# Turning rows ahead of their norm, halves for the first expert's rows, VectorE in place of GpSimd for low halves, and unread products in TensorE's waits

## What is computed

```
xn = rms_norm(x, norm2_g)
g_logits = xn @ wg + bg                      # 4 groups
g_idx = argmax(g_logits); g_w = softmax(g_logits)[g_idx]
e_logits = (xn @ we + be)[group g_idx]       # 4 experts of that group
top_p, top_i = top_k(softmax(e_logits), 2); top_p /= sum(top_p)
y = sum over the two experts e of g_w * top_p * ((silu(xn @ w_gate[e]) * (xn @ w_up[e])) @ w_down[e])
out = rms_norm(x + y, final_norm_g)
```

## Time and profile before

| | |
|---|---|
| median of 3 runs | 869.72 us |
| profiled execution | 869.15 us, span 867.4 us |
| TensorE busy | 801.0 us (92%) |
| VectorE busy | 495.5 us (57%) |
| ACT busy | 449.2 us (52%) |
| POOL busy | 218.0 us (25%) |
| granted TensorE clock, mean | 0.965 |
| TensorE in the chain that ended last | 81% |

### The profile page before, as it was taken

The page is one execution under the profiler, slowest core; times in us unless marked ns, Lnnn a source line. Parts: engine busy times, 40 slices in busy tenths (PEclk is TensorE's granted clock), DMA queues, the critical chain, the costliest instruction groups (busy, mean ns, idle before and its releaser), DMA issues.

```text
span 867.4 us, 10612 instructions
## 1 busy us (share of the span) xinstructions
PE 801.0 (92%) x3635; PEld 631.7 (73%) x3635; DVE 495.5 (57%) x649; ACT 449.2 (52%) x580; POOL 218.0 (25%) x126
## 2 busy tenths in 40 slices
PE   4999999999979999999999967899999999999960
PEld 3887766676756888888888866688787787877750
DVE  6613647657472222204012435698889898988865
ACT  5244637454552232323222221687888878887842
POOL 5554323132232344444444234000000000000013
PEclk9999999999999999999999967999999999999995
DMA  8665451512120343333328364999999999975945
GB/s 308 179 243 188 128 194 49 194 49 74 40 80 27 89 169 118 99 93 95 98 96 280 131 239 197 366 400 385 405 389 393 408 395 406 389 299 209 367 137 207
DMA packets 126633, 186.76 MB, mean 215 GB/s; under 512 B 9149, under 2 KB 61957, under 8 KB 126597
## 3 DMA queue, kind: packets, MB, share of 16 engines
q1 hardware_dynamic: 119156, 167.82, 54.3%
q10 hardware_dynamic: 5136, 10.08, 3.1%
q0 software_dynamic: 2304, 8.39, 2.7%
HBM read 158.99 MB, written 27.28 MB: 215 GB/s over the span
## 4 chain that ended last, share of the span: by engine, by line
PE 81%; DVE 7%; ACT 4%; issue 3%; DMA 2%; POOL 1%; ACTq 1%; DVEq 0%; SPq 0%
PE ps L947 24%; PE ps L949 23%; PE ps L948 23%; PE ps L1030 3%; PE ps L1010 2%; PE ps L1171 2%; PE ps L1019 1%; DVE w_lo L350 1%; PE ps L1119 1%; ACT w_hi L339 1%; DVE rgate L1394 1%; PE ps L1178 1%; DMA x<-in_x 1%; ACT xn L879 1%; DMA slots<-y_tile 1%
## 5 line engine op out<-in xcount | busy, mean ns | idle before, releaser
L344 POOL TENSOR_TENSOR w_lo<-raw,w_hi 128x1024 fp32r<-128x1024 f32 x72 | 176.2, 2450 | 286.8 <-ACT w_hi L332 286.8
L332 ACT ACTIVATE w_hi<-raw 128x1024 fp32r<-128x1024 f32 x73 | 77.0, 1057 | 169.0 <-PE ps L949 159.9
L947 PE MATMUL ps<-xn_hi,w_hi 128*128 128x512 f32 x352 | 143.8, 409 | 0.0
L949 PE MATMUL ps<-xn_hi,w_lo 128*128 128x512 f32 x352 | 137.5, 390 | 0.0
L948 PE MATMUL ps<-xn_lo,w_hi 128*128 128x512 f32 x352 | 137.3, 390 | 0.0
L947 PE MATMUL ps<-w_hi,xT_hi 128*128 128x512 f32 x256 | 105.2, 411 | 8.1 <-DVE xT_lo L1644 5.5
L948 PE MATMUL ps<-w_lo,xT_hi 128*128 128x512 f32 x256 | 102.3, 399 | 0.0
L949 PE MATMUL ps<-w_hi,xT_lo 128*128 128x512 f32 x256 | 102.2, 399 | 0.0
L947 PEld LDWEIGHTS ps<-xn_hi,w_hi 128*128 128x128 f32 x352 | 66.0, 188 | 26.8 <-issue 13.8
L614 POOL DMA_INDIRECT raw_mg<-slots,slot_idx x7 | 6.9, 982 | 303.6 <-ACTq L930 295.1
L949 PEld LDWEIGHTS ps<-xn_hi,w_lo 128*128 128x128 f32 x352 | 66.1, 188 | 14.4
(11 more groups left out here) (260 smaller groups left out, 1457.5 us busy)
## 6 DMA issues: line engine op xcount, KB each, us to landing
raw<-in_w_in SPq DMA_DIRECT2D x52, 512.0 KB, 3.7
raw_mg<-in_exp_w_down SPq DMA_DIRECT2D x36, 512.0 KB, 8.3
raw<-in_exp_w_gate SPq DMA_DIRECT2D x28, 512.0 KB, 10.3
raw_a<-in_exp_w_gate SPq DMA_DIRECT2D x27, 512.0 KB, 9.8
raw_c<-in_exp_w_up SPq DMA_DIRECT2D x27, 512.0 KB, 9.2
slots<-raw SPq DMA_DIRECT2D x24, 512.0 KB, 6.5
raw_mg<-in_exp_w_up SPq DMA_DIRECT2D x21, 512.0 KB, 9.8
raw<-in_exp_w_up SPq DMA_DIRECT2D x16, 512.0 KB, 9.5
```

The lines of the kernel that those rows point to most:

```text
L332: nc.scalar.activation(w_hi[:, b % HI_SLOTS, :], raw_buf(b), ACT.Copy)\
L344: eng.tensor_tensor(w_lo[:, b % HI_SLOTS, :], raw_buf(b), w_hi[:, b % HI_SLOTS, :].bitcast(F32), ALU.subtract)\
L947: pe.matmul(dst, hi_l, hi_r, start=start, stop=False)
L949: return pe.matmul(dst, lo_l, hi_r, start=False, stop=stop)
```

## The change

1. The rows are turned ahead of their norm. `turn_x2(t)` turns x_rows (not xn2) as soon as x is added, in the middle of the products of tile t+1, and logits(t) follows tile t+1 of w_out. So that the logits come out right, router_w is multiplied by norm2_g once (VectorE, ahead of the additions, from a new load `g2_cols` on ACT's queue), and the logits are multiplied by each row's factor in one more operation. VectorE waits for all six of ACT's loads of the semaphore route_in there.
2. The bookkeeping. The two subtractions for the exponentials and the table of experts stand later in VectorE's list. `picked_bf` comes from one addition. The weights of the choices (`weights`) stand behind the experts.
3. Low halves. POOL makes none for the experts; blocks 0 to 3 of the first expert go to VectorE, behind its routing. SP's fetches of blocks 0 to 2 of tile 2 wait for them there.
4. Tile 0 in halves. The matrix of zeros and ones is made in four operations, one for each token tile. The gathering is made in two halves of four k each, and high and low parts follow in halves; the first two blocks of the expert wait only for the first half's.
5. Unread products. After the last logits 11, after the counts 2, and before and after `turn_x(x_odd)` 8 each, products of the identity by itself (128 x 128 x 128, float32) go into bank 7.

```diff
@@ SP
                 if r == 3:
+                    sp.wait_ge(S["tile0_half"], 2)
                     sp.wait_ge(S["scattered"], 16 * 2 * NT)
@@ POOL
-            for r in range(AHEAD):
-                split_lo(pool, B_EXP + r)
...
-            for r in range(AHEAD, 8 + AHEAD):
-                if r < 8:
-                    if on_pool(r):
-                        split_lo(pool, B_EXP + r)
@@ ACT
                     act.dma_start(g2_rows[:, :], a["norm2_g"][0:1, :].broadcast_to([P, D])).then_inc(S["g2_in"], 16)
+                    act.dma_start(g2_cols[:, :], a["norm2_g"][0].rearrange("(k p) -> p k", p=P),
+                                  allow_slow_non_contiguous=True)\
+                       .then_inc(S["route_in"], 16)
                     act.dma_start(router_w[:, :, 0:NG], a["router_grp_w"][0].rearrange("(k p) n -> p k n", p=P))\
...
-            xT_hi_part(1)
+            act.wait_ge(S["gexp_in"], 1)
+            act.activation(route[:, 4, 0:4 * NG], route[:, 3, 0:4 * NG], ACT.Exp).then_inc(S["gexp_done"], 1)
+            act.wait_ge(S["gexp_in"], 2)
+            act.activation(route[:, 12, :], route[:, 11, :], ACT.Exp).then_inc(S["eexp_done"], 1)
+            for half in range(2):
+                act.wait_ge(S["tile0_half"], half + 1)
+                act.activation(xT_hi[:, 4 * half:4 * half + 4, :].rearrange("p k n -> p (k n)"),
+                               ps[:, 3 + half, :], ACT.Copy).then_inc(S["tile0_hi"], 1)
@@ TensorE
+            def turn_x2(t):
+                pe.wait_ge(S["x2_done"], NT + t + 1)
...
+                                      x_rows[:, t, k * P:(k + 1) * P], ident[:, :])
...
-                if t >= 2:
-                    logits(t - 2)
+                    if kp == 1 and t >= 1:
+                        turn_x2(t - 1)
                 if t >= 1:
-                    turn_xn2(t - 1)
-            turn_xn2(NT - 1)
-            logits(NT - 2)
+                    logits(t - 1)
+            def unread(n):
+
+                for _ in range(n):
+                    pe.matmul(ps[:, 7, 0:P], ident[:, :], ident[:, :], start=True, stop=True)
+
+            turn_x2(NT - 1)
             logits(NT - 1)
+            unread(11)
...
             mm.then_inc(S["counts_ps"], 1)
+            unread(2)
...
+            for half in range(2):
                 for t in range(NT):
...
+                    if half == 0:
+                        pe.wait_ge(S["tile0_where"], t + 1)
+                    for k in range(4 * half, 4 * half + 4):
+                        mm = pe.matmul(ps[:, 3 + half, (k % 4) * P:(k % 4 + 1) * P], xn2[:, t, k * P:(k + 1) * P],
...
             for r in range(8):
+                pe.wait_ge(S["tile0_lo"], 1 if r < 2 else 2)
                 lo_wait(pe, B_EXP + r)
                 expert_block(r % HI_SLOTS, r // 4, 2 * (r % 4), KD, xT_hi, xT_lo)
+            unread(8)
             turn_x(x_odd, S["x_odd_in"], 16)
+            unread(8)
@@ VectorE
             dve.wait_ge(S["g2_in"], 16)
+            dve.wait_ge(S["route_in"], 96)
+            dve.tensor_tensor(router_w[:, :, :], router_w[:, :, :],
+                              g2_cols[:, :].unsqueeze(2).to_broadcast([P, KD, NG + NE]), ALU.mult)\
+               .then_inc(S["router_scaled"], 1)
...
-                                   router_b[:, :].unsqueeze(1).to_broadcast([P, NT, NG + NE]), ALU.add))
+                                   stat[:, 5, :].unsqueeze(2).to_broadcast([P, NT, NG + NE]), ALU.mult))
+            link(dve.tensor_tensor(both, both, router_b[:, :].unsqueeze(1).to_broadcast([P, NT, NG + NE]), ALU.add))
...
+            for t in range(NT):
+                dve.tensor_scalar(silu[:, t * P:(t + 1) * P], hid[:, 0:P], slot0[:, t:t + 1], None, ALU.is_equal)\
+                   .then_inc(S["tile0_where"], 1)
+            dve.tensor_tensor(row(11, NT, NE), e_log, spread(e_max, NT, NE), ALU.subtract).then_inc(S["gexp_in"], 1)
...
+            for half in range(2):
+                split_lo(dve, B_EXP + half)
+                dve.wait_ge(S["tile0_hi"], half + 1)
+                dve.tensor_tensor(xT_lo[:, 4 * half:4 * half + 4, :].rearrange("p k n -> p (k n)"), ps[:, 3 + half, :],
+                                  xT_hi[:, 4 * half:4 * half + 4, :].rearrange("p k n -> p (k n)").bitcast(F32),
+                                  ALU.subtract).then_inc(S["tile0_lo"], 1)
+            dve.sem_inc(S["xT_done"], 1)
+            for r in range(2, 8):
+                split_lo(dve, B_EXP + r)
             for r in range(8, 8 + AHEAD):
...
+                split_lo_loop(dve, at_odd(0), r - 8)
+            tables()
+            xT_lo_part(2)
             hidden(B_EXP + 8, 1)
-            xT_lo_part(2)
```

More of the change, by code:

```diff
@@ L79 @@
 SLOT_TILES = MAX_TILES + 1
-def on_pool(r):
-    return r < 4
 LO_DVE_0 = 32
-def pool_before(r):
-    return sum(on_pool(x) for x in range(r))
 def build(nc, a, out):
@@ L192, in build @@
             router_b = sb(s2, "router_b", [P, NG + NE])
-            sb(s2, "to_line", [P, 8])
+            g2_cols = sb(s2, "g2_cols", [P, KD])
             xT_hi = sb(s2, "xT_hi", [P, KD, P], F32R)
@@ L351, in split_lo_loop @@
                               w_hi[:, (8 + r) % HI_SLOTS, :].bitcast(F32), ALU.subtract)\
-               .then_inc(S["lo_pool"] if on_pool(8 + r) else S["lo_dve"], 1)
+               .then_inc(S["lo_dve"], 1)
         def pair_block(j, r):
@@ L1614, in _ @@
             dve.tensor_copy(idx[:, :, 1:2], s_second.unsqueeze(2)).then_inc(S["routed"], 1)
-            link(dve.tensor_scalar(late[:, 0, 0:1], upto[:, NE - 1:NE], float(NE - PAIRED + 1), None, ALU.add))
-            dve.tensor_copy(tile_table[:, 0:1], late[:, 0, 0:1])
-            dve.tensor_copy(tile_table[:, 1:NE + 1], count16)
-            over = row(18, 8, NE)
-            link(dve.tensor_tensor(over, upto.unsqueeze(1).to_broadcast([P, 8, NE]),
-                                   count8.unsqueeze(2).to_broadcast([P, 8, NE]), ALU.is_le))
@@ L1623, in _ @@
-            dve.wait_ge(S["gexp_done"], 1)
-            link(dve.tensor_reduce(row(3, 8), over, AX.X, ALU.add))
-            link(dve.tensor_scalar(row(3, 8), row(3, 8), float(NE - 1), None, ALU.min))
-            dve.tensor_copy(tile_table[:, NE + 1:NE + 9], row(3, 8)).then_inc(S["tab"], 1)
-            comb = row(12, NT, NE)
-            dve.wait_ge(S["eexp_done"], 1)
-            link(dve.tensor_tensor(comb, comb, sel1, ALU.mult))
-            link(dve.tensor_reduce(e_sum, comb, AX.X, ALU.add))
@@ L1632, in _, with tables @@
-            link(dve.tensor_reduce(g_sum, row(4, NT, NG), AX.X, ALU.add))
-            link(dve.tensor_tensor(scale_t, g_sum, e_sum, ALU.mult))
-            link(dve.reciprocal(scale_t, scale_t))
-            link(dve.tensor_tensor(comb, comb, spread(scale_t, NT, NE), ALU.mult))
-            for k, s in enumerate((s_first, s_second)):
-                link(dve.tensor_tensor(late, slot, spread(s, NT, NE), ALU.is_equal))
-                link(dve.tensor_tensor(late, late, comb, ALU.mult))
-                link(dve.tensor_reduce(w_first[:, k, :], late, AX.X, ALU.add))
+            def tables():
+                link(dve.tensor_scalar(slot0[:, 0:1], upto[:, NE - 1:NE], float(NE - PAIRED + 1), None, ALU.add))
+                dve.tensor_copy(tile_table[:, 0:1], slot0[:, 0:1])
+                dve.tensor_copy(tile_table[:, 1:NE + 1], count16)
+                over = row(18, 8, NE)
+                link(dve.tensor_tensor(over, upto.unsqueeze(1).to_broadcast([P, 8, NE]),
+                                       count8.unsqueeze(2).to_broadcast([P, 8, NE]), ALU.is_le))
+                link(dve.tensor_reduce(row(10, 8), over, AX.X, ALU.add))
+                link(dve.tensor_scalar(row(10, 8), row(10, 8), float(NE - 1), None, ALU.min))
+                dve.tensor_copy(tile_table[:, NE + 1:NE + 9], row(10, 8)).then_inc(S["tab"], 1)
@@ new lines, in weights @@
+            def weights():
+                dve.wait_ge(S["gexp_done"], 1)
+                comb = row(12, NT, NE)
+                dve.wait_ge(S["eexp_done"], 1)
+                link(dve.tensor_tensor(comb, comb, sel1, ALU.mult))
+                link(dve.tensor_reduce(e_sum, comb, AX.X, ALU.add))
+                link(dve.tensor_reduce(g_sum, row(4, NT, NG), AX.X, ALU.add))
+                link(dve.tensor_tensor(scale_t, g_sum, e_sum, ALU.mult))
+                link(dve.reciprocal(scale_t, scale_t))
+                link(dve.tensor_tensor(comb, comb, spread(scale_t, NT, NE), ALU.mult))
+                for k, s in enumerate((s_first, s_second)):
+                    link(dve.tensor_tensor(late, slot, spread(s, NT, NE), ALU.is_equal))
+                    link(dve.tensor_tensor(late, late, comb, ALU.mult))
+                    link(dve.tensor_reduce(w_first[:, k, :], late, AX.X, ALU.add))
@@ L1673, in tile @@
                 for r in range(PER_TILE):
-                    if not on_pool(8 + r + AHEAD):
-                        split_lo_loop(dve, at, r + AHEAD)
+                    split_lo_loop(dve, at, r + AHEAD)
```

(4 more changed lines are left out.)

79 lines of the change are left out of this document (16 added, 63 removed).

## The result

The changed kernel took 889.6 us (median of 4 runs, 887.59 to 890.21), the kernel before 870.21 us beside it (4 runs, 869.38 to 871.4). The ratio is 1.0218, with a 95% interval of 1.0196 to 1.0239: 2.2% slower. The forecast was 865.9 with a range of 861.5 to 871. The profiled execution took 890.13 us, with a span of 888.4.

What follows compares the result with a forecast made beforehand. The routing stretch (505 to 558 us) was taken as improvable, its gain limited by the second expert's rows landing. Summed delays and savings moved that expert's start from 555.1 to 551.3: 3.8 us off 869.72 gives 865.9, range 861.5 to 871.

Steps and rivals of the forecast that it cites:

- (2): Last tiles of w_out: rows turned before their norm, +2.7 us before its last products end, then 5.5 for 12.9.
- A to C: From the end of w_out's last products to VectorE's return with the counts: 12.2 us forecast, before 20.7.
- (1): ACT's queue before w_out's additions: the g2_cols load adds 4.6 us of waiting, delaying the first addition 3.1.
- Rival (b): ACT's queue has room for the new load, so no delay: 3.1 us less, 862.8; chance 18%.
- rival (e): 4-byte pieces drain at half speed; ACT's issue waits 11.6 us in place of 4.6: 872.9; chance 6%.
- (3): VectorE's routing, logits to counts: 5.15 us in place of 7.1, with 1.66 gone with POOL's splits.
- (4): From the counts to the second expert's rows landing: 0.3 us for comparisons and subtraction, 3.2 for three loads inside the scatter.
- rival (d): VectorE's splits hold up POOL's eight scatter issues; scatter ends 9.8 us later in place of 3.2: 872.5; chance 13%.
- Rival (c): The third tile's three loads do not delay the scatter: 3.2 us less, 862.7; chance 10%.
- (5): First expert: halves remove 2.68 us of waiting, but the gain is lost waiting 2.5 to 5.4 for the second rows.
- (6): Second expert starts 4.8 us after its rows land, at 551.3 in place of 555.1; `weights` hidden at the end.
- Rival (f): The clock falls at both places and the queue drains fully (1.2 + 0.8 + 1.2): 869.1, no difference; chance 8%.

Runs made afterwards that it cites:

- copy first: The changed kernel with ACT's copy of the previous tile's turned rows put ahead of the square of the current tile: 870.81 us, ratio 0.9999 to the kernel before.

## Why the prediction was wrong

It named the direction wrongly, by one step, and that step is (2), "Rows turned ahead of their norm". It priced the new set of logits of each tile in w_out at its own 1.7 us and the turn at 1.04, +2.7 before A. It took for granted that the copied rows would be there when the logits want them. The copy stands on ACT behind the next tile's square, which waits for the end of the next tile's products. The wait was to be found before the run, by asking what is queued ahead of ACT's copy: (2) counted a copy on the path for the last tile alone (1.0 and 0.1), and none for the logits that follow the products of tiles 1, 2 and 3. In the step's place the runs showed +17.0 us from the first addition to A, and from A to C 7.1 more than with the two entries exchanged. With them exchanged it was +2.9 to A, for +2.7 forecast.

The steps, one by one:

(1) *The load*: mechanism right, size off. Priced as 4.6 of ACT's waiting and 3.1 until the first addition; measured 5.7 (14.56 less 8.88) and 4.6. That is near the upper bound that the prediction kept, "by draining" (5.8 and 4.3). Rival (b), room in the queue, is excluded by the load added to the kernel before, and rival (e), an issue wait of 11.6, by the 5.7. But the reason given for 5.8 does not carry over: in the changed kernel the router's two loads landed at 478.7 and 479.9, 1.2 us apart and not 5.8 (issued at 462.08 and 463.06, 16.6 and 16.8 to landing). What ACT's issues wait for is open. That the load costs by its place, and little at the end, was not foreseen.

(2) *Before A*: failed, above. *Behind A* and (3): 12.2 forecast from A to C; 18.8 measured in the changed kernel, of which 2.9 are the wait that stands there for tile 2 and 4.2 the low clock (the two sets of logits 3.60 in place of 1.85 and 1.96, the turn 1.95 in place of 1.07); 11.7 with the copy first. So the shorter chain and the POOL stall that went were priced rightly. The stall itself: (3) put 1.66 us on it, which it was before the change; with the denser chain the same three splits of POOL cost 4.75 when they were given back.

(4) *C to X*: 3.5 forecast for what is added, 4.8 measured, 5.5 with the copy first. The three loads cost 2.7 (3.2 forecast), the comparisons and the subtraction 0.3 as forecast, and two issues beside VectorE's splits last 1.0 longer each, which is rival (d) at a fifth of its size (2.0 of 9.8). Over all kernels every issue behind the first that lasts longer than 0.96 lies beside a split, but not every issue beside a split is long. That the splits cause it is argued from this alone; what picks the issues is open. Rival (c), no delay by the loads, is excluded.

(5) *First expert*: right that nothing is gained, and the run without the overlap shows it. TensorE waited 6.5 us for the second rows in place of 2.5 to 5.4, because C to X was 1.2 longer than forecast.

(6) *Second expert*: right: 4.5 from X, 4.8 forecast, and from there on 312.2, 312.3 forecast. The clock did fall for the turn (1.97) and was back for the expert. But not every execution of the kernel before has the 1.6 us of low clock that were to be won there: with the load added it began the second expert at full clock, without unread products. `weights` stayed hidden at the end.

Had (2) been priced with its wait, the sum would have been slower than before, whatever the clock: three waits of 2.9, against a forecast gain of 3.8. From the first addition to C the exchange gave back 21.2 us (14.1 and 7.1 in the table). The waits are 8.7 of them; the other 12.5 are the low clock behind them. The span fell by 19.3 and the median by 18.8, since C to X and the start to P0 came out 1.9 longer. Rival (f) had the clock falling, but at places and sizes that made no difference in all.

## What to carry to other kernels

When an operation is moved earlier on one engine, read the in-order list of each engine that feeds it: the operand is produced where that list stands, not where its data is ready. Here the exchange of two neighbouring entries on ACT was worth 18.8 us of 889.6. A wait of TensorE can be dearer than its length, because the work behind it may run at the lower clock: here 8.7 us of waits brought 12.5 us of low clock. Where such a wait can't be removed, products into an unread bank can hold the clock: here they were worth 2.3 us. A load of a thousand small pieces cost 4.6 us in front of others on its queue, 0.7 as the last of them, and nothing that could be seen far ahead of its use.

## What the hardware showed that was not expected

Two issues on ACT's queue stood for 6.35 and then 5.41 us behind loads of 1024 pieces each, and one such load of 4 KB, in pieces of 4 bytes, added 5.7 us of waiting. The same load as the last of seven took 0.65 us to issue. In the kernel before, the scatter's issues all took 0.95 us but for the first; beside VectorE's splits of 128x1024 some take 1.96. And the last tile's logits, behind the same wait of 1.11 us, took 1.96, 2.65, 3.06, 3.14, 3.50 or 3.60 us in one execution each of kernels that differ only elsewhere: whether the clock falls there could not be tied to anything that these runs varied.
